# Gate groups of a routed-expert stage: one 256-column matmul per token, hi and lo parts side by side, seven tokens to a group

## What is computed

```python
def one_block(xb):
    q = (xb @ w_query).reshape(PEER_BLOCK, PEER_HEADS, 2, D_KEY_HALF)
    s = jnp.einsum('thpk,hpnk->thpn', q, sub_keys).astype(jnp.float32)
    s_top, i_top = lax.top_k(s, PEER_TOPK)
    cand = s_top[:, :, 0, :, None] + s_top[:, :, 1, None, :]
    cand_idx = i_top[:, :, 0, :, None] * N_KEYS + i_top[:, :, 1, None, :]
    ...
    best, pos = lax.top_k(cand, PEER_TOPK)
    idx = jnp.take_along_axis(cand_idx, pos, axis=-1)
    g = jax.nn.softmax(best, axis=-1)
    u = expert_u[idx]
    v = expert_v[idx]
    a = jax.nn.gelu(jnp.einsum('td,thkd->thk', xb, u))
    return jnp.einsum('thk,thkd->td', (g * a.astype(jnp.float32)).astype(v.dtype), v)
```

## Time and profile before

| | us |
|---|---|
| median of 3 runs | 4294.23 |
| lowest and highest | 4292.34, 4297.27 |
| the profiled execution's own time | 4291.41 |
| its span, first to last instruction | 4289.7 |
| TensorE busy, of the span | 4120.7 |
| VectorE busy | 2747.5 |
| ScalarE busy | 1337.7 |
| GpSimd busy | 1022.3 |

### The profile page before, as it was taken

The page is one execution under the profiler, slowest core; times in us unless marked ns, Lnnn a source line. Parts: engine busy times, 40 slices in busy tenths (PEclk is TensorE's granted clock), DMA queues, the critical chain, the costliest instruction groups (busy, mean ns, idle before and its releaser), DMA issues.

```text
span 4289.7 us, 78346 instructions
## 1 busy us (share of the span) xinstructions
PE 4120.7 (96%) x30416; PEld 4003.8 (93%) x30416; DVE 2747.5 (64%) x4349; ACT 1337.7 (31%) x1967; POOL 1022.3 (24%) x793
## 2 busy tenths in 40 slices
PE   7999999899999999999989999899999999999998
PEld 3898988899999999999979899899999999999998
DVE  2268438966766626777753774597667664377776
ACT  2221323333333333333332123333333333333332
POOL 0054000000122205565310720000002221255551
PEclk9999999999999999999999999999999999999999
DMA  4443222354445558999834432215444555599994
GB/s 171 131 114 128 99 100 68 103 163 135 126 172 175 176 193 281 351 346 354 332 116 109 117 111 80 73 59 167 139 134 144 173 177 211 184 345 348 351 346 181
DMA packets 305045, 781.13 MB, mean 182 GB/s; under 512 B 36272, under 2 KB 159536, under 8 KB 302432
## 3 DMA queue, kind: packets, MB, share of 16 engines
q1 hardware_dynamic: 176640, 441.70, 31.2%
q10 hardware_dynamic: 81120, 196.10, 12.7%
q0 software_dynamic: 47104, 141.00, 9.2%
HBM read 655.79 MB, written 122.88 MB: 182 GB/s over the span
## 4 chain that ended last, share of the span: by engine, by line
PE 88%; DVE 8%; issue 1%; ACT 1%; DMA 1%; DVEq 0%; ACTq 0%; SPq 0%; POOLq 0%
PE pg L1408 18%; PE pg L1411 17%; PE pg L1409 17%; PE pm L1692 4%; PE pg L1694 4%; PE pm L1694 4%; PE pm L1693 4%; PE pg L1693 4%; PE pg L1692 4%; PE pm L1651 4%; PE pm L1454 3%; DVE pick_i L1222 1%; DVE pick_i L1214 1%; DVE score_r L1215 1%; DVE ys L1097 1%
## 5 line engine op out<-in xcount | busy, mean ns | idle before, releaser
L1408 PE MATMUL pg<-a_hi,w_hi 128*128 128x260 f32 x6400 | 1702.9, 287 | 77.2 <-DVE w_lo L912 17.1
L1409 PE MATMUL pg<-a_lo,w_hi 128*128 128x260 f32 x6400 | 1679.2, 284 | 0.4 <-issue 0.4
L912 DVE TENSOR_TENSOR w_lo<-raw,w_hi 128x1024 fp32r<-128x1024 f32 x688 | 864.4, 1258 | 1171.4 <-ACT w_hi L822 738.6
L1408 PEld LDWEIGHTS pg<-a_hi,w_hi 128*128 128x128 f32 x6400 | 1219.3, 191 | 94.8 <-issue 62.5
L1411 PE MATMUL pg<-a_hi,w_lo 128*128 128x260 f32 x6400 | 1296.6, 284 | 0.0
L1409 PEld LDWEIGHTS pg<-a_lo,w_hi 128*128 128x128 f32 x6400 | 1217.9, 190 | 0.8 <-issue 0.5
L1411 PEld LDWEIGHTS pg<-a_hi,w_lo 128*128 128x128 f32 x6400 | 993.6, 190 | 0.0
L822 ACT CAST w_hi<-raw 128x1024 fp32r<-128x1024 f32 x508 | 534.0, 1051 | 785.8 <-PE pg L1694 636.2
L529 POOL DMA_INDIRECT rows<-stream,at_v x256 | 282.7, 1104 | 771.0 <-DVE acc_tok L1340 314.7
L577 ACT ACTIVATE hid<-pg 128x260 f32<-128x260 f32 x512 | 170.7, 385 | 945.4 <-PE pg L1411 942.6
L539 POOL TENSOR_TENSOR one_j<-one_j,g_lo 128x1024 fp32r<-128x1024 f32 x98 | 186.1, 1899 | 1079.5 <-DVEq L1318 1079.5
(11 more groups left out here) (226 smaller groups left out, 5785.1 us busy)
## 6 DMA issues: line engine op xcount, KB each, us to landing
raw<-stream SPq DMA_DIRECT2D x688, 512.0 KB
hidden_dram<-hid SPq DMA_DIRECT2D x256, 196.0 KB, 3.5
gate_dram<-gate_buf ACTq DMA_DIRECT2D x14, 3584.0 KB, 11.7
hid_in<-hidden_dram ACTq DMA_DIRECT2D x64, 784.0 KB
gate_in<-gate_dram ACTq DMA_DIRECT2D x64, 784.0 KB
ada_raw<-stream ACTq DMA_DIRECT2D x80, 512.0 KB, 3.3
hid_tok<-hid SPq DMA_DIRECT2D x256, 64.0 KB, 3.5
rows<-stream,at_v POOLq DMA_INDIRECT x256
```

What stands on the lines that cost most here:

```text
L912: tt(ring(False, s), raw[:, s], ring(True, s).bitcast(F32), ALU.subtract).then_inc(lo_ready, 1)
L1408: pe.matmul(outs[h], w[0], a[h][0], start=first, stop=False)
L1409: pe.matmul(outs[h], w[0], a[h][1], start=False, stop=False)
```

## The change

A gate group has seven tokens instead of eight, so there are 56 groups per layer in place of 49, in blocks 60 to 115 (G_END = 116). Per token one matmul streams both parts of `one_j` side by side, 256 columns; nothing is added in PSUM. Seven tokens take 3.5 of the four banks of `pm`, and the groups no longer alternate: TensorE waits for the group before to be taken. ScalarE copies the half from part 0 into `gate_buf`, at the head of the next block, ahead of `read_product`; VectorE then adds the half from part 1, after the one-hots and ahead of the split of that block. `gate_buf` is now two halves of 28 tokens (GB = 28), each stored after four groups, so 14 stores per layer, one block later and after ScalarE's cast. `gate_dram` keeps the order that the group loads read, so a store writes runs of 112 values (448 B). The group loads stay as long and as many; the first two are issued at block 120 instead of 113.

In the diff the first `take_gates` is ScalarE's, the second VectorE's.

```diff
-GS = 8
-GB = 56
+GS = 7
+GB = 28
...
-    gate_dram = nc.dram_tensor("gate_dram", (GBN, P, NBLK, GB), F32).ap()
+    gate_dram = nc.dram_tensor("gate_dram", (GBN // 2, P, NBLK // 4, 2, 4 * GB), F32).ap()
...
-        gate_buf = sb(gs, "gate_buf", [P, NBLK, GB])
+        gate_buf = sb(gs, "gate_buf", [P, 2, NBLK, GB])
...
+        gate_parts = pm[:, :, :].rearrange("p b (t z j) -> p j z (b t)", t=2, z=2)
+
+        def gates_of(n):
+
+            m, k = divmod(n, GB // GS)
+            return gate_buf[:, m % 2, :, k * GS:(k + 1) * GS]
...
                 def take_gates(n):
+                    m, k = divmod(n, GB // GS)
                     act.wait_ge(g_prod, l * NSUB + (n + 1) + 2)
-                    if n % (GB // GS) == 0:
-
-                        act.wait_ge(g_out, (l * GBN + n // (GB // GS)) * 16 + 1)
-                    t0 = n % (GB // GS) * GS
-                    for q in range(2):
-                        own.do(act.copy(gate_buf[:, :, t0 + 4 * q:t0 + 4 * q + 4],
-                                        pm[:, 2 * (n % 2) + q, :].rearrange("p (t j) -> p j t", t=4)))
-                    own.settle()
-                    act.sem_inc(g_free, 1)
-                    if n % (GB // GS) == GB // GS - 1:
-                        act.sem_inc(passed, 1)
-                        act.dma_start(gate_dram[n // (GB // GS)].rearrange("p j t -> p (j t)"),
-                                      gate_buf[:, :, :].rearrange("p j t -> p (j t)")).then_inc(g_out, 16)
+                    if k == 0:
+                        act.wait_ge(g_out[m % 2], (l * (GBN // 2) + m // 2) * 16 + 1)
+                    own.link(act.copy(gates_of(n), gate_parts[:, :, 0, 0:GS]))
+                    act.sem_inc(gate_hi_taken, 1)
+
+                def store_gates(m):
+                    act.wait_ge(g_free, l * NSUB + (m + 1) * (GB // GS) + 1)
+                    act.sem_inc(passed, 1)
+                    act.dma_start(gate_dram[m // 2][:, :, m % 2, :], gate_buf[:, m % 2].rearrange("p (g j) t -> p g (j t)", j=4)
+                                  ).then_inc(g_out[m % 2], 16)
...
                 for block in range(NBLK):
                     s = block % 4
 
+                    if G_FROM < block <= G_END:
+                        take_gates(block - G_FROM - 1)
...
-                    elif block < G_END:
-                        take_gates(block - G_FROM)
+                    if block - G_FROM - 1 in range(GB // GS, NSUB + 1, GB // GS):
+                        store_gates((block - G_FROM - 1) // (GB // GS) - 1)
...
+                def take_gates(n):
+                    dve.wait_ge(gate_hi_taken, l * NSUB + (n + 1))
+                    to = gates_of(n)
+                    own.link(tt(to, gate_parts[:, :, 1, 0:GS], to, ALU.add))
+                    dve.sem_inc(g_free, 1)
...
                     if G_FROM <= block < G_END - 1:
                         one_hots(block - G_FROM + 1)
+                    if G_FROM < block <= G_END:
+                        take_gates(block - G_FROM - 1)
                     split(l, T_EU + 4 + block, block % 4)
...
                     for t in range(GS):
-                        for z in range(2):
-                            mm = pe.matmul(pm[:, 2 * (n % 2) + t // 4, (t % 4) * P:(t % 4 + 1) * P], one_i[:, n % 2, t, :],
-                                           one_j[:, n % 2, z, t, :], start=z == 0, stop=z == 1)
+                        mm = pe.matmul(pm[:, t // 2, t % 2 * 2 * P:(t % 2 + 1) * 2 * P].rearrange("p (z j) -> p z j", z=2),
+                                       one_i[:, n % 2, t, :], one_j[:, n % 2, :, t, :], start=True, stop=True)
```

More of the change, by code:

```diff
@@ L343, in build @@
         hid_out = [sem(f"hid_out{s}") for s in range(4)]
-        one_ready, g_prod, g_free, g_out = (sem(n) for n in ("one_ready", "g_prod", "g_free", "g_out"))
-        ghi_of_picks, one_lo_ready = sem("ghi_of_picks"), sem("one_lo_ready")
+        one_ready, g_prod, g_free = (sem(n) for n in ("one_ready", "g_prod", "g_free"))
+        g_out = [sem("g_out0"), sem("g_out1")]
+        ghi_of_picks, one_lo_ready, gate_hi_taken = sem("ghi_of_picks"), sem("one_lo_ready"), sem("gate_hi_taken")
         at_ready = sem("at_ready")
@@ L353, in build @@
         y_fin, y_done = sem("y_fin"), sem("y_done")
-        counts_from_one = [mod_taken, lo_ready, *pg_free, s_prod, s_copied, *hid_out, g_out, rt_ready, rt_prod]
-        counts_from_two = [g_free, g_prod]
+        counts_from_one = [mod_taken, lo_ready, *pg_free, s_prod, s_copied, *hid_out, *g_out, g_free, rt_ready, rt_prod]
+        counts_from_two = [g_prod]
         own_act, own_dve, own_pool = sem("own_act"), sem("own_dve"), sem("own_pool")
@@ L832, in load_group @@
                     act.dma_start(hid_to[:, :, :], hidden_dram[:, 4 * g:4 * g + 4, :]).then_inc(down_in[g % 3], 16)
-                    act.dma_start(gate_to[:, :, :], gate_dram.rearrange("b p j t -> p b (j t)")[:, :, 4 * g * GB:4 * (g + 1) * GB]
+                    act.dma_start(gate_to.rearrange("p (b z) x -> p b (z x)", z=2), gate_dram.rearrange("b p g z x -> p g b (z x)")[:, g]
                                   ).then_inc(down_in[g % 3], 16)
                 def take_gates(n):
+                    m, k = divmod(n, GB // GS)
                     act.wait_ge(g_prod, l * NSUB + (n + 1) + 2)
-                    if n % (GB // GS) == 0:
-                        act.wait_ge(g_out, (l * GBN + n // (GB // GS)) * 16 + 1)
-                    t0 = n % (GB // GS) * GS
-                    for q in range(2):
-                        own.do(act.copy(gate_buf[:, :, t0 + 4 * q:t0 + 4 * q + 4],
-                                        pm[:, 2 * (n % 2) + q, :].rearrange("p (t j) -> p j t", t=4)))
-                    own.settle()
-                    act.sem_inc(g_free, 1)
-                    if n % (GB // GS) == GB // GS - 1:
-                        act.sem_inc(passed, 1)
-                        act.dma_start(gate_dram[n // (GB // GS)].rearrange("p j t -> p (j t)"),
-                                      gate_buf[:, :, :].rearrange("p j t -> p (j t)")).then_inc(g_out, 16)
+                    if k == 0:
[7 more added lines that the diff above has]
+                                  ).then_inc(g_out[m % 2], 16)
                 for block in range(NBLK):
                     s = block % 4
+                    if G_FROM < block <= G_END:
+                        take_gates(block - G_FROM - 1)
                     act.wait_ge(hid_out[s], (l * (NBLK // 4) + block // 4) * 32 + 1)
@@ L873, in _ @@
                             act.sem_inc(ghi_of_picks, 1)
-                    elif block < G_END:
-                        take_gates(block - G_FROM)
+                    if block - G_FROM - 1 in range(GB // GS, NSUB + 1, GB // GS):
+                        store_gates((block - G_FROM - 1) // (GB // GS) - 1)
                     if block == G_END + 4:
-                        act.wait_ge(g_out, (l + 1) * (16 * GBN) + 1)
+                        for z in range(2):
+                            act.wait_ge(g_out[z], (l + 1) * (16 * GBN // 2) + 1)
                         for s in range(4):
@@ L1702, in _ @@
                 buffer(l, G_ED // 2, 1)
-                pe.wait_ge(g_free, (l + 1) * NSUB + 2)
+                pe.wait_ge(g_free, (l + 1) * NSUB + 1)
                 pe.sem_inc(passed, 1)
```

## The result

| | before | after |
|---|---|---|
| median of 18 runs, us | 4294.67 | 4301.57 |
| lowest and highest | 4288.20, 4297.27 | 4292.26, 4307.98 |
| profiled execution: its time, its span | 4291.41, 4289.7 | 4300.16, 4298.2 |

The ratio is 1.0017, with a 95% interval from 1.0011 to 1.0023: the change makes the kernel 6.9 us slower, where 2.2 us faster was forecast. That is inside the range and within the 0.2% that was called no change, but on the other side of zero, and the 18 runs tell it from zero.

The account below looks back on a forecast made before the run. TensorE was taken to bound the gate stage; per layer 17.6 + 26 x 14.53 plus two blocks of 6.57 made 408.5 against 409.6 us, -2.2 in all, hence 4292 us; 8-in-10 range 4266 to 4372.

Parts of the forecast that it names:

- The two-block loop through one set of banks: Gate blocks: product read, cast, split, one-hots, add, next gates close a loop of 14.53 us, blocks of 6.57 and 7.96.
- The other pointers: Signs: 784 matmuls of 128x256, TensorE waiting 27 times a layer, 70 to 80 us, add 1.09, stores 7 to 18.
- the sum: Gate stage per layer: 409.6 us before against 408.5 after, so -1.1 a layer and -2.2 in all.
- The way from the add to TensorE and its restart: End of the two-block chain: 0.13 us to the other engine, 0.2 to restart, 0.82 for seven gate matmuls.
- the split's 1.22: VectorE's split in the two-block chain: forecast at 1.14 us, starting 1.93 after ScalarE begins to read the product.
- the one-hots' 3.28: VectorE's three one-hots in the two-block chain: forecast at 3.22 us, followed by a gap of 0.15.
- The last two blocks: End of the gate stage, where the one-hots have run out: two blocks of 6.57 us.
- The first two blocks: Start of the gate stage: 17.6 us, with one TensorE wait of 3.8 us for the first add.
- Before: Stage in the kernel before, per layer: 49 x 7.515 + 7 x 5.752 + 1.1 for the first wait = 409.6 us.
- TensorE keeps the pace: Rival, gate stage: the add comes before TensorE needs the banks, 56 x 6.57 us, 4212 us in all; chance 9%.
- The dearer add: Rival, VectorE's add: at 2.0 us the total is 4341, standing still for GpSimd 4372; chance 14%.
- The store: Rival, gate stores: 4096 short rows hold ScalarE's queue or land late, 4393 or about 4550 us; chance 12%.

Follow-up runs that it names:

- one-hot last: Changed kernel with the first one-hot of the next group written after VectorE's add instead of first: 4248.48 us, ratio 0.9889 to the kernel before.
- cast first: Changed kernel with ScalarE casting the tile for VectorE's split before it reads the product in the gate blocks: 4254.23 us, ratio 0.9900 to the kernel before.
- two matmuls: Changed kernel with two matmuls of 128 columns per token again, side by side in the same banks: 4366.65 us, ratio 1.0109 to the kernel before.
- the same cast on the kernel before: Kernel before, with ScalarE's cast ahead of its read of the product in the gate blocks: 4314.52 us, ratio 0.9994 to the unedited kernel before.
- both orders: Changed kernel with ScalarE's cast ahead of its product read and the first one-hot written after the add: 4218.09 us, ratio 0.9818 to the kernel before.
- no add: Changed kernel without VectorE's add of the second gate part, ScalarE's copy freeing the banks: 4234.87 us, ratio 0.9802 to the kernel before.
- add first with a small GpSimd product: Changed kernel with VectorE's add ahead of the one-hots and GpSimd multiplying the low part of one token in seven: 4215.48 us, ratio 0.9812.
- the small product: Changed kernel with GpSimd multiplying the low part of only one token in seven: 4298.33 us, ratio 1.0004 to the kernel before.
- long rows: Changed kernel with each gate store written in one row of 14 KB a partition instead of 32 of 448 bytes: 4325.37 us, ratio 1.0013.

## Why the prediction was wrong in its sign

**The mechanism was right.** The two-block loop through one set of banks was forecast at 14.53 us, alternating 6.57 and 7.96; it takes 14.64, alternating 6.57 and 8.07. Shortening it by 0.93 or 0.92 us (one-hot last, cast first) or lengthening it by 0.74 (two matmuls) moved the total by the pairs times that, and the same cast on the kernel before moved nothing. The other pointers held: 784 matmuls of 256 columns, the add at 1.09 us beside GpSimd's product, ScalarE's copy at 0.985, stores landing in 10.7 us. TensorE waited 60 times and 67.0 us, where 54 times and 70 to 80 us were forecast.

**The step that failed is the sum**, -2.2 us the small difference of two stages of some 409 us. Four of its terms were mis-sized.
- *The way from the add to TensorE and its restart.* Forecast 0.13, then 0.2 + 0.82. In the chain TensorE starts 0.20 after the add's end (1172.57 to 1172.77) and its group takes 1.07. The 0.13 had been read from VectorE to GpSimd, an engine that idled; no row of before showed VectorE releasing TensorE in this place. Together 0.12, all of the 14.64 against 14.53; the split's 1.22 for 1.14 and the one-hots' 3.28 for 3.37 make up for each other. The first layer's 26 pairs sum to 380.5, 2.7 us more than the forecast 377.8; the second's to 381.4, 3.6 more, three of its pairs being 0.3 longer, for a reason that I did not look for. So +6.3.
- *The last two blocks.* Forecast at TensorE's 6.57 each; they take 7.21 + 6.58 and 6.87 + 6.57, as the chain still holds the first of them: +0.9.
- *The first two blocks.* Forecast 17.6, from one wait of 3.8 us. They take 15.92 and 17.48. The wait is 2.5 us in both layers: -1.8. The wait had been worked out with product 60 as early as in the first layer of before, where it is read 5.04 us after the one-hots begin (1146.57 and 1141.53); here it is read 6.56 after them (1149.12 and 1142.56), because of the step told of below; 3.8 less these 1.5 is 2.3, near the 2.5 measured. The second layer's 17.48 holds 1.56 us of half clock, told in the last section.
- *Before.* Both layers were counted with a 1.1 us wait at the first gate group. The second has none (408.43 against 409.6): +1.2 on the difference.

6.3 + 0.9 - 1.8 + 1.2 = 6.6; with the forecast -2.2 that is +4.4, against +4.55 counted off in the stage. The working had the price of such errors, 5.3 us for each 0.1 us in the chain, and with it the range was right; the likeliest value lay nearer to zero than the terms were known.

**The step outside the stage's sum** was not forecast: block 59 to 60 took 1.5 us more in the first layer. Busy time there, before and after, clock third from the end:

```profile
1137.75:1146.57 8.82, 6.15 (x50) 5.79 (x48) 6.55 (x6) 2.54 (x6) 1.27 (x1) 1.00 0.51 134
```

```profile
1138.77:1149.12 10.35, 7.78 (x53) 7.63 (x52) 8.08 (x7) 2.53 (x5) 1.68 (x1) 0.84 0.40 122
```

The clock differs, 1.00 against 0.84, and before has the same 10.31 us step in its own second layer. It is no effect of the change: before's first layer is the exception. The profiles kept of the thirteen kernels here have this step 26 times, each time behind a wait of TensorE of 2.6 us; 25 times, the kernel before with the cast first included, the clock over it is 0.83 to 0.85, and the step 10.31 to 10.40 us (11.23 to 11.28 where the read comes behind the cast). Whether the +2.4 us elsewhere are more than scatter is open: the changed kernel's 18 runs span 16 us, and no run here was made for it.

**The rivals.** TensorE keeps the pace: no, but both orders, no add, and add first with a small GpSimd product each reach it, at 0.980 to 0.982 of before, where the forecast for that pace was 4212 us, 0.981. The dearer add: no, 1.082 to 1.098 us in 112 executions, so VectorE reads PSUM in steps of 1 KB at the rate of plain rows, and GpSimd doesn't stop it. GpSimd does stop VectorE's split (2.75 us beside it, 1.23 without), as it stopped the one-hot of the earlier trace rows (2.62 us at the start of the changed kernel's stage, 1.33 with the small product). This agrees with the rule in the Trainium skill, SBUF — State Buffer, section Who interferes with whom, by which a VectorE instruction with two inputs in SBUF contends and one with a single input there does not. The store: no, its issue takes 0.53 us where 1 to 4 were feared, and long rows gave nothing back. The Trainium skill, DMA: Bandwidth & Descriptors, section Specifications, asks for rows of 512 B; the landing of 10.7 us against 6.5 is on its side, and costs nothing here.

## What to carry over

A change that frees time on the bound engine by giving up a double buffer closes a loop: add up that loop, over as many blocks as it spans, before counting the gain. Here the single matmul was worth 80 us, and 83 were lost to an add that stands behind a cast, a split and three one-hots. What stands in such a loop is found by asking what must end before the buffer is released. The cure was order, not less work: whatever isn't needed for the release goes behind it, on the idle-looking ScalarE as well, until the loop is shorter than the bound engine's own time. When a forecast is a difference of two nearly equal sums, links of 0.1 us decide its sign.

## What the runs showed of the hardware

After a wait of 2.54 us TensorE ran part of one product at half rate, its lower level of 1.2 GHz. TensorE's timeline in the second layer, and the window of that block:

```profile
3254.59 1.07 PE L1667 MATMUL pm<-one_j,one_i 128*128 128x256 f32 x7 [2.54 <-DVEq L1333]
3255.49 0.28 PE L1425 MATMUL pg<-a_hi,w_hi 128*128 128x260 f32 x1
3255.61 0.28 PE L1426 MATMUL pg<-a_lo,w_hi 128*128 128x260 f32 x1
...
3256.49 0.42 PE L1425 MATMUL pg<-a_hi,w_hi 128*128 128x260 f32 x1
3256.70 0.42 PE L1426 MATMUL pg<-a_lo,w_hi 128*128 128x260 f32 x1
```

```profile
3252.20:3263.10 10.90, 8.51 (x58) 8.54 (x59) 7.75 (x7) 2.78 (x5) 3.37 (x2) 0.84 0.41 125
```

Matmuls start 0.12 apart at first, then 0.21 apart for some 3 us, and the block takes 10.91. The same block of the first layer, after a wait as long, kept the full clock:

```profile
1155.69:1165.04 9.35, 6.90 (x58) 6.93 (x59) 7.81 (x7) 2.79 (x5) 3.37 (x2) 1.00 0.49 144
```

So a wait of this length costs 1.56 us more in one place and nothing in another of the same run, with the same instructions around it. It doesn't look like mere chance: in the kernels with the cast first and with long rows too, where the wait is again 2.5 to 2.6 us, the third block kept 1.00 in the first layer and had 0.84 in the second. Nor does the length of the wait settle it. With two matmuls TensorE waits only 1.8 us there, and the clock over the block is 0.84 in both layers; with the first one-hot last it waits 1.7 us, and the clock stays at 1.00 in both. What else decides, no run here shows.
